# The last two down-projection tiles, the norm and the next mixer's first three tiles in halves of 128 tokens

## The chip, the cores and the metric

The kernel runs on one core of a Trainium2 chip. The metric is the time of one execution on the device in microseconds (us); several executions are timed and their median is compared.

## The reference, cut to what matters

A sequence of 256 tokens with 1024 channels goes through two stacks. The first (two blocks) is not touched. The second ("second layer" in the title) has four blocks, each a mixer and a feed-forward part, both followed by a residual and a layer norm:

```python
def swiglu(x, w_in, w_down):
    gate, up = jnp.split(x @ w_in, 2, axis=-1)
    return (jax.nn.silu(gate) * up) @ w_down

for i in range(4):                      # gated delta net, hgrn2, gla, gated delta net
    m = mixer_i(x)                      # begins with x @ w_in
    x = layer_norm(DN_ALPHA * x + m, mix_ln_g[i], mix_ln_b[i])
    x = layer_norm(DN_ALPHA * x + swiglu(x, ffn_w_in[i], ffn_w_down[i]), ffn_ln_g[i], ffn_ln_b[i])
return x
```

The hidden width is 2816, so the down projection contracts 22 blocks of 128 rows. The layer norm takes mean and variance over the 1024 channels of each token, so tokens are independent of each other in it. All is float32.

## The kernel before, in words

Activations are held transposed: channels on the 128 partitions, tokens along the free axis. `X` holds the residual stream as 8 channel tiles (`KC` = 8) of 256 tokens (`T`), `Xs` its split into a rounded part and a remainder in the reduced float32 type (float32r), 8 tiles each.

Every large projection is done by output tiles of 128 channels. `pe_block` (L595) makes one contraction block of one output tile with three matmuls: high weights by high activations (L597), high weights by low (L598), low weights by high (L599). Each matmul brings its own 128x128 weight load and streams 256 tokens. Weights arrive by DMA in `raw` (four slots, queue of SyncE), ScalarE rounds them to `w_hi` (L560, `split_hi`), VectorE subtracts to `w_lo` (L566, `split_lo`); both work some pieces ahead of TensorE.

`pe_ffn` (L690 on) does 44 up tiles and then the 8 down tiles; a down tile is 22 blocks in three pieces of 8, 8 and 6 (`PARTS`), so 66 matmuls. As each tile ends, VectorE adds the residual (`dve_residual`, L916), ScalarE squares it (L782), VectorE sums tiles and squares (L893, L897). After the last tile `pe_stats` multiplies these sums by a matrix of ones (L665, L666), then the last tile and its squares (L669, L671), in full float32. `pe_warm` issues five matmuls whose result nobody reads (L676), in the first three blocks only. Then `dve_ln` and `act_ln` (L843 to L881) form mean and reciprocal deviation and run a pipeline over the 8 channel tiles: centre (L849), scale (L853), gain and bias on ScalarE (L880 into `Xs`, L881 into `X`), remainder on VectorE (L870), which signals `h_ready` for one tile.

The next mixer begins with `pe_group`: its first three output tiles (`AHEAD` = 3) are advanced together, block k of all three as soon as `h_ready` has come for k, 72 matmuls in all. Its fourth tile follows when `lo_ready` says that its weights are split. After the last block ScalarE's queue stores the whole output with one DMA (L2940).

Three places join a feed-forward part to a mixer (blocks 0, 1 and 2); the fourth ends the program.

Of the kernel before, what the change touches and what calls it, by code (L numbers as in the profile page):

```python
# [147 lines left out]
def build(nc, a, out, stop=None):  # L148
    with ExitStack() as ctx:
# [19 lines left out]
        X = sb("X", [P, KC, 2 * T])  # L169
        M = sb("M", [P, KC, T])  # L170
        R = sb("R", [P, 8, 512])
        W = sb("W", [P, 8, 512])
        VC, NV = vector_columns()
        vec = sb("vec", [P, NV])
        ident, ones, halves, swap = (sb(n, [P, P]) for n in ("ident", "ones", "halves", "swap"))
        rope_cos, rope_sin = sb("rope_cos", [P, T]), sb("rope_sin", [P, T])
# [176 lines left out]
        for name, n, kind in plan:  # L353
# [4 lines left out]
            kinds += [kind] * n  # L358

        @block.sync  # L360
        def _(sp):
# [13 lines left out]
            for name, first, n, kind in [(name, *run, kind) for name, n, kind in plan for run in ORDER.get(name, ((0, n),))]:  # L375
# [156 lines left out]
        class Ahead:  # L532
# [21 lines left out]
        def split_hi(act, slot, fresh=False):  # L554
            if slot is None:
                return
            act.wait_ge(*loaded[slot].due("act", 16))
            if not fresh:
                act.wait_ge(*gemm_out.seen("act"))
            nc.scalar.activation(w_hi[:, slot], raw[:, slot], ACT.Identity).then_inc(*hi_ready.inc())  # L560

        def split_lo(dve, slot):
            if slot is None:
                return
            dve.wait_ge(*hi_ready.due("dve"))
            nc.vector.tensor_tensor(w_lo[:, slot], raw[:, slot], w_hi[:, slot], ALU.subtract).then_inc(*lo_ready.inc())  # L566

# [28 lines left out]
        def pe_block(to, w_slot, k, x_hi, x_lo, start, stop):  # L596
            nc.tensor.matmul(to, w_hi[:, w_slot, k, :], x_hi, start=start, stop=False)  # L597
            nc.tensor.matmul(to, w_hi[:, w_slot, k, :], x_lo, start=False, stop=False)  # L598
            return nc.tensor.matmul(to, w_lo[:, w_slot, k, :], x_hi, start=False, stop=stop)  # L599

# [15 lines left out]

        def pe_features(pe, tiles, n, ready=None):
# [8 lines left out]
            peel = SLOTS if ready or tiles == SLOTS else 0  # L626
            if ready:
                pe_group(pe, 0, n, ready)
            for u in range(AHEAD if ready else 0, peel):
# [60 lines left out]
        def pe_ffn(pe, n, stats, layer_norm=False, warm=5):  # L690
# [181 lines left out]
        def act_ln(act, which, i, split=True):  # L872
# [3 lines left out]
            for m in range(KC):  # L876
# [1085 lines left out]

        def pe_gdn(pe, i, ready):
            chunk = lambda t: slice(t * P, (t + 1) * P)
# [100 lines left out]

            pe_group(pe, 0, T, ready)
            for n in range(AHEAD, len(GDN_TILES)):
# [677 lines left out]

        def pe_hgrn(pe, ready):
            z = hgrn_
            pe_features(pe, 24, T, ready)
# [85 lines left out]

        def pe_gla(pe, ready):
            z = gla_
            pe_features(pe, 8, T, ready)
            for k in range(KC):
# [49 lines left out]
        @block.tensor  # L2888
        def _(pe):
            pe.wait_ge(*const_made.due("pe", 4))  # L2890
            pe_first(pe)
            if "ev_in" in names:
                pe_even(pe)
            if "up0" in names:
                pe_ffn0(pe)
            if "od_in" in names:
                pe_odd(pe)
            if "up1" in names:
                pe_ffn(pe, T, 0)
            for i, mixer in second:  # L2900
                if f"{mixer}_in" in names:
                    {"hgrn": pe_hgrn, "gla": pe_gla}.get(mixer, lambda e, r: pe_gdn(e, i // 3, r))(pe, pe_h(pe))
                if f"up_2_{i}" in names:
                    pe_ffn(pe, T, T, layer_norm=True, warm=5 if i < 3 else 0)

        @block.scalar
        def _(act):
# [21 lines left out]
            for i, mixer in second:  # L2929
# [4 lines left out]
                if f"up_2_{i}" in names:  # L2934
                    act_ffn(act, None, T)
                    act_squares(act, T, 3)
                    act_ln(act, "ffn", i, i < 3)
            if stop is None:
                act.wait_ge(*affine.sent())
                act.dma_start(out, Xl).then_inc(*stored.inc(16))  # L2940
                act.wait_ge(*stored.sent())

        @block.vector
        def _(dve):
# [29 lines left out]
            for i, mixer in second:  # L2974
# [123 lines left out]
```

## Time and profile before

| what | value |
|---|---|
| median of 3 runs | 2551.23 us (2549.55 to 2552.09) |
| profiled execution: first to last instruction (span) | 2545.7 us |
| median less that span | 5.5 us |
| TensorE matmuls busy | 2464.1 us, 97% |
| TensorE weight loads busy | 2261.9 us, 89% |
| VectorE, ScalarE busy | 1769.0 us, 1179.2 us |
| mean granted clock of TensorE | 0.988 |

The profiled execution has no time of its own beside its span; the 5.5 us are what the runs hold around the first and last instruction. PE is TensorE's matmuls, PEld its weight loads. A matmul in float32 appears as two records, each with a weight load of its own; one in float32r appears as one. Durations of matmuls overlap, so the pace of a stream is read from the distance between starts. The granted clock is 1.0 at 2.4 GHz and 0.5 at 1.2 GHz.

### The profile page before, as it was taken

Reading aid. Unit: us, or ns where it says so; the run is one execution under the profiler, and the core shown is the slowest. Engines: PE = TensorE matmul, PEld = TensorE weight load, DVE = VectorE, ACT = ScalarE, POOL = GpSimd, SP = SyncE. Lnnn points to the kernel's source line nnn. Section 1 sums busy time; section 2 is a strip of 40 time slices with the busy share of each in tenths; the row PEclk is TensorE's granted clock in tenths of the full one; section 3 lists DMA queues with packets and bytes.
Section 4 is the critical chain, followed back from the end, with each engine's and each line's share of the span. In section 5 each row is a group of like instructions: output and inputs, shape, how many; then the busy total and the mean of one; then the engine's idle time right before and its main releaser. Section 6 shows DMA issues by size and latency. Waiting matters only on the chain.

```text
span 2545.7 us, 46612 instructions
## 1 busy us (share of the span) xinstructions
PE 2464.1 (97%) x17610; PEld 2261.9 (89%) x17610; DVE 1769.0 (69%) x2863; ACT 1179.2 (46%) x1816; POOL 105.9 (4%) x161
## 2 busy tenths in 40 slices
PE   8999999999999999989999999999989999989998
PEld 6866777778798999988999998999989999988997
DVE  5878699988747866675665767666457657766665
ACT  4554421223545444455544544544545446455443
POOL 2221000000000000003000000000000000000000
PEclk9999999999999999999999999999999999999999
DMA  7323255554424554321555431555415554222553
GB/s 296 141 104 137 100 182 186 183 182 154 167 92 148 191 181 162 112 84 67 173 182 189 159 108 67 181 181 183 157 51 177 186 179 152 100 75 75 198 178 121
DMA packets 119641, 378.13 MB, mean 149 GB/s; under 512 B 11592, under 2 KB 29000, under 8 KB 119121
## 3 DMA queue, kind: packets, MB, share of 16 engines
q1 hardware_dynamic: 105936, 327.58, 38.1%
q0 software_dynamic: 12528, 47.62, 5.4%
q8 instruction: 94, 1.54, 0.2%
q10 hardware_dynamic: 1040, 1.05, 0.1%
q14 instruction: 43, 0.34, 0.0%
HBM read 375.15 MB, written 1.05 MB: 148 GB/s over the span
## 4 chain that ended last, share of the span: by engine, by line
PE 85%; DVE 9%; ACT 4%; issue 2%; DMA 0%; DVEq 0%; ACTq 0%; SPq 0%
PE gb L597 22%; PE gb L598 21%; PE gb L599 21%; DVE w_lo L566 3%; PE mb L676 2%; PE mb L2636 2%; PE gb L1162 1%; ACT w_hi L560 1%; PE gb L2617 1%; PE gb L2132 1%; PE mb L2150 1%; PE mb L599 1%; PE mb L598 1%; PE mb L597 1%; DVE W L2372 1%
## 5 line engine op out<-in xcount | busy, mean ns | idle before, releaser
L597 PE MATMUL gb<-Xs,w_hi 128*128 128x256 f32 (+1 forms) x3584 | 1098.3, 306 | 18.1 <-DVE w_lo L566 5.2
L599 PE MATMUL gb<-Xs,w_lo 128*128 128x256 f32 (+1 forms) x3584 | 1083.3, 302 | 0.0
L598 PE MATMUL gb<-Xs,w_hi 128*128 128x256 f32 (+1 forms) x3504 | 1053.4, 301 | 0.0
L560 ACT ACTIVATE w_hi<-raw 128x1024 fp32r<-128x1024 f32 x616 | 646.6, 1057 | 775.8 <-PE gb L599 730.6
L566 DVE TENSOR_TENSOR w_lo<-raw,w_hi 128x1024 fp32r<-128x1024 f32 x616 | 747.7, 1225 | 222.6 <-ACT w_hi L560 215.6
L597 PEld LDWEIGHTS gb<-Xs,w_hi 128*128 128x128 f32 x3584 | 679.0, 189 | 73.6 <-issue 29.9
L599 PEld LDWEIGHTS gb<-Xs,w_lo 128*128 128x128 f32 x3584 | 678.5, 189 | 31.2
L598 PEld LDWEIGHTS gb<-Xs,w_hi 128*128 128x128 f32 x3504 | 664.3, 190 | 26.4 <-issue 1.2
L598 PE MATMUL gb<-Fs,w_hi 128*128 128x256 f32 (+1 forms) x1016 | 294.4, 290 | 0.0
L597 PE MATMUL gb<-Fs,w_hi 128*128 128x256 f32 (+1 forms) x936 | 263.2, 281 | 0.0
L599 PE MATMUL gb<-Fs,w_lo 128*128 128x256 f32 (+1 forms) x936 | 261.9, 280 | 0.0
L598 PEld LDWEIGHTS gb<-Fs,w_hi 128*128 128x128 f32 x1016 | 190.9, 188 | 4.3 <-issue 0.2
L597 PEld LDWEIGHTS gb<-Fs,w_hi 128*128 128x128 f32 x936 | 175.8, 188 | 0.6 <-issue 0.2
L599 PEld LDWEIGHTS gb<-Fs,w_lo 128*128 128x128 f32 x936 | 175.9, 188 | 0.4
L994 ACT ACTIVATE W<-W 128x512 f32<-128x512 f32 (+1 forms) x44 | 23.1, 526 | 224.4 <-DVE W L953 224.4
L1269 DVE CUSTOM_DVE_ANT_0 R<-R,M 128x1024 f32<-128x1024 f32 x74 | 92.7, 1253 | 2.6
L1269 DVE CUSTOM_DVE_ANT_0 W<-R,M 128x1024 f32<-128x1024 f32 x74 | 92.3, 1248 | 0.1
L916 DVE SCALAR_TENSOR_TENSOR X<-X,gb 128x256 f32<-128x256 f32 x64 | 26.7, 417 | 92.0 <-PE gb L599 91.8
L2372 DVE SCALAR_TENSOR_TENSOR W<-gb,vec,W 128x255 f32<-128x255 f32 x96 | 46.1, 480 | 38.6 <-ACT W L2295 36.9
L964 DVE TENSOR_TENSOR W<-W,gb 128x256 f32<-128x256 f32 x110 | 46.1, 419 | 37.4 <-PE gb L599 37.2
L782 ACT ACTIVATE W<-X 128x256 f32<-128x256 f32 (+1 forms) x88 | 39.5, 448 | 63.5 <-DVE X L916 41.7
L474 POOL DMA_DIRECT2D R<-in_mod_later x80 | 42.6, 534 | 463.5 <-DVE modv L1273 395.0
(402 smaller groups left out, 2889.9 us busy)
## 6 DMA issues: line engine op xcount, KB each, us to landing
raw<-in_up SPq DMA_DIRECT2D x264, 512.0 KB, 3.8
raw<-in_down SPq DMA_DIRECT2D x96, 512.0 KB, 3.6
R<-in_mod_later POOLq DMA_DIRECT2D x80, 512.0 KB, 3.9
raw<-in_gdn_in SPq DMA_DIRECT2D x64, 512.0 KB, 3.6
raw<-in_down SPq DMA_DIRECT2D x48, 384.0 KB, 3.9
raw<-in_hgrn_in SPq DMA_DIRECT2D x32, 512.0 KB, 3.9
raw<-in_ev_in SPq DMA_DIRECT2D x24, 512.0 KB, 5.3
raw<-in_gla_in SPq DMA_DIRECT2D x24, 512.0 KB, 4.1
```

The source lines that it names most:

```text
L474: pool.dma_start(mod_ring[u], (a["mod_later"][t] if isinstance(t, int) else a["mod_later"][bass.ds(t, 1)].rearrange("a p n -> p (a n)"))). ...
L560: nc.scalar.activation(w_hi[:, slot], raw[:, slot], ACT.Identity).then_inc(*hi_ready.inc())
L566: nc.vector.tensor_tensor(w_lo[:, slot], raw[:, slot], w_hi[:, slot], ALU.subtract).then_inc(*lo_ready.inc())
L597: nc.tensor.matmul(to, w_hi[:, w_slot, k, :], x_hi, start=start, stop=False)
L598: nc.tensor.matmul(to, w_hi[:, w_slot, k, :], x_lo, start=False, stop=False)
L599: return nc.tensor.matmul(to, w_lo[:, w_slot, k, :], x_hi, start=False, stop=stop)
L676: nc.tensor.matmul(mb[:, 0, :], ones[:, :], vec[:, 0:512], start=True, stop=True)
L782: nc.scalar.activation(squares_at(m, n) if m else sq_sum(n), X[:, m, 0:n], ACT.Square, scale=1 / 32).then_inc(*sq_ready.inc())
L964: link(dve, nc.vector.tensor_tensor(g, g, bb, ALU.mult))
L1269: last = nc.vector.tensor_tensor_reduce(mod_ring[u] if s else product, mod_ring[u], c_rows[:, s, :], 1.0, 0.0, ALU.mult, ALU.add, sums[:, ...
L2372: link(dve, nc.vector.scalar_tensor_tensor(out=t[:, 3 - k:T], in0=a[:, 0:T - 3 + k], scalar=tap[k], in1=t[:, 3 - k:T], op0=ALU.mult, op1=A ...
L2636: last = nc.tensor.matmul(bank[:, b * 64:(b + 1) * 64], keys[:, b, :], queries[:, b * 64:(b + 1) * 64], start=True, stop=True)
```

## The change

In each feed-forward part of the second stack, down tiles 0 to 5 stay as they are. Tiles 6 and 7 (`HALVED`) are made for tokens 0 to 127 first (66 matmuls of 128 tokens each), then for tokens 128 to 255 (again 66 each). The split weights of both tiles must therefore be kept until the second pass: five of their six pieces (`ASIDE`) go to unused memory instead of the four slots. The statistics, the norm and the residual are done by halves (`stats`, `dve_ln_half`, `act_ln_half`), the first half's after four blocks of tile 6's second half. The norm walks over channels in chunks of 2, 2 and 4 tiles. The next mixer's first three tiles are done as 72 matmuls for the first half and 72 for the second (`pe_group_halves`), with the second half's statistics after the first two blocks. The five unread matmuls are gone from these places. The output is stored in four DMAs from SyncE's queue, two for each half. The first layer's parts and the norms after the mixers are not touched.

The diff, cut to its core (one level of indentation removed):

```diff
+HALVED = (KC - 2, KC - 1)
+ASIDE = (18, 21, 20, 22, 23)
+first_of = {name: sum(p[1] for p in plan[:j]) for j, (name, _, _) in enumerate(plan)}
+aside_of = {first_of[f"down_2_{i}"] + t: SLOTS + e for i in range(4) if f"down_2_{i}" in first_of for e, t in enumerate(ASIDE)}
+pairs = lambda z: z.rearrange("p (r b) n -> p r b n", b=2)
+def weights_at(w, part):
+    if w < SLOTS:
+        return (w_hi, w_lo)[part][:, w]
+    if w < SLOTS + 2:
+        return Rr[:, 2 * (w - SLOTS) + part]
+    if w == SLOTS + 2:
+        return spent[:, :, :] if part else Fs[:, FC:FC + 2, :].rearrange("p r (b n) -> p (r b) n", n=P)[:, 0:FC - WIDE]
+    r = 8 * (w - SLOTS - 3) + 4 * part
+    return Xs[:, r:r + 4, T:2 * T].rearrange("p r (b n) -> p r b n", b=2)
...
+    if stop is None:
+        for h in range(2):
+            for j in range(2):
+                cols, rows = slice(h * P, (h + 1) * P), slice(4 * j, 4 * j + 4)
+                sp.wait_ge(*final_made.due("sp", 1 if j else 2))
+                sp.dma_start(out[:, rows, cols], X[:, rows, cols]).then_inc(*stored.inc(16))
+        sp.wait_ge(*stored.sent())
...
+def pe_group_halves(pe, stats):
+    for u in range(AHEAD):
+        pe.wait_ge(*lo_ready.due("pe"))
+        pe.wait_ge(*gemm_taken.free("pe"))
+    for h, cols in enumerate(SIDES):
+        for k in range(KC):
+            pe.wait_ge(*h_ready.due("pe"))
+            for u in range(AHEAD):
+                last = pe_block(gb[:, u, cols], u, k, Xs[:, k, cols], Xs[:, KC + k, cols], k == 0, k == KC - 1)
+                if h and k == KC - 1:
+                    last.then_inc(*gemm_out.inc())
+            if h == 0 and k == 1:
+                stats(1)
...
+def pe_stats_half(pe):
+    def stats(h):
+        cols = SIDES[h]
+        pe.wait_ge(*sums_kept.due("pe"))
+        nc.tensor.matmul(mb[:, 2, cols], ones[:, :], x_sum[:, cols], start=True, stop=False)
+        nc.tensor.matmul(sbank[:, cols], ones[:, :], sq_sum(T)[:, cols], start=True, stop=False)
+        pe.wait_ge(*(gemm_taken.seen("pe", pe_next["tiles"]) if h else half_taken.due("pe")))
+        nc.tensor.matmul(mb[:, 2, cols], ones[:, :], X[:, KC - 1, cols], start=False, stop=True).then_inc(*mean_done.inc())
+        pe.wait_ge(*sq_ready.due("pe", 2 if h else KC))
+        nc.tensor.matmul(sbank[:, cols], ones[:, :], squares_at(KC - 1, T)[:, cols], start=False, stop=True).then_inc(*sum_done.inc())
+    return stats
+pe_next = {"tiles": 0}
+def pe_ffn_halves(pe, last_stage):
+    stats = pe_stats_half(pe)
+    pe_features(pe, 2 * FC, T, pe_h(pe))
+    def part_of(m, part, cols, first, end):
+        t = 3 * m + part
+        w = SLOTS + ASIDE.index(t) if t in ASIDE else t % SLOTS
+        for b in range(first, end):
+            k = KC * part + b
+            if m == 0:
+                pe.wait_ge(*gemm_taken.seen("pe", 2 * FC + 1 - 2 * (k + 1)))
+            last = pe_block(gb[:, m % BANKS, cols], w, b, hid[:, 0, k, cols], hid[:, 1, k, cols], k == 0, k == FC - 1)
+        return last
+    for m in range(KC):
+        pe.wait_ge(*gemm_taken.free("pe"))
+        for part, blocks in enumerate(PARTS):
+            pe.wait_ge(*lo_ready.due("pe"))
+            last = part_of(m, part, SIDES[0] if m in HALVED else slice(0, T), 0, blocks)
+            if m not in HALVED:
+                last.then_inc(*gemm_out.inc())
+        if m in HALVED:
+            last.then_inc(*half_out.inc())
+    for m in HALVED:
+        if m == HALVED[0]:
+            pe.wait_ge(*half_taken.due("pe"))
+        for part, blocks in enumerate(PARTS):
+            if m == HALVED[0] and part == 0:
+                part_of(m, part, SIDES[1], 0, 4)
+                stats(0)
+                last = part_of(m, part, SIDES[1], 4, blocks)
+            else:
+                last = part_of(m, part, SIDES[1], 0, blocks)
+            last.then_inc(*gemm_out.inc())
+    if last_stage:
+        pe_next["tiles"] = 0
+        stats(1)
+    pe_next["tiles"] = AHEAD
+    return stats
...
+CHUNKS = (slice(0, 2), slice(2, 4), slice(4, KC))
+def dve_ln_half(dve, h, split, beside=None):
+    cols, kept_cols = SIDES[h], slice(T + SIDES[h].start, T + SIDES[h].stop)
+    dve.wait_ge(*mean_done.due("dve"))
+    link(dve, nc.vector.tensor_scalar(W[:, 2, kept_cols], mb[:, 2, cols], 1.0 / D, None, ALU.mult))
+    nc.vector.tensor_tensor(W[:, 2, cols], W[:, 2, kept_cols], W[:, 2, kept_cols], ALU.mult).then_inc(*dve_step.inc())
+    dve.wait_ge(*sum_done.due("dve_sum"))
+    dve.wait_ge(*dve_step.sent())
+    nc.vector.tensor_tensor(W[:, 3, cols], sbank[:, cols], W[:, 2, cols], ALU.subtract).then_inc(*moments.inc())
+    spread = lambda z, ms: z.unsqueeze(1).broadcast_to([P, ms.stop - ms.start, P])
+    for ms in CHUNKS:
+        nc.vector.tensor_tensor(work[:, ms, cols], X[:, ms, cols], spread(W[:, 2, kept_cols], ms), ALU.subtract).then_inc(*centred.inc())
+    dve.wait_ge(*rstd_ready.due("dve"))
+    for ms in CHUNKS:
+        dve.wait_ge(*centred.due("dve"))
+        nc.vector.tensor_tensor(work[:, ms, cols], work[:, ms, cols], spread(W[:, 3, kept_cols], ms), ALU.mult).then_inc(*normed.inc())
+    for j, ms in enumerate(CHUNKS):
+        if beside and j == len(CHUNKS) - 1:
+            beside()
+        if split:
+            dve.wait_ge(*affine.due("dve"))
+            lo = slice(KC + ms.start, KC + ms.stop)
+            nc.vector.tensor_tensor(Xs[:, lo, cols], X[:, ms, cols], Xs[:, ms, cols], ALU.subtract).then_inc(*h_ready.inc(ms.stop - ms.start))
+def act_ln_half(act, i, h, split, beside=None):
+    cols, kept_cols = SIDES[h], slice(T + SIDES[h].start, T + SIDES[h].stop)
+    act.wait_ge(*moments.due("act"))
+    alink(act, nc.scalar.activation(W[:, 3, cols], W[:, 3, cols], ACT.Ln, bias=eps[:, 1:2]))
+    nc.scalar.activation(W[:, 3, kept_cols], W[:, 3, cols], ACT.Exp, scale=-0.5).then_inc(*rstd_ready.inc())
+    for j, ms in enumerate(CHUNKS):
+        if beside and j == len(CHUNKS) - 1:
+            beside()
+        act.wait_ge(*normed.due("act"))
+        for m in range(ms.start, ms.stop):
+            last = nc.scalar.activation(X[:, m, cols], work[:, m, cols], ACT.Identity, bias=vcol("ffn_b", KC * i + m),
+                                        scale=vcol("ffn_g", KC * i + m))
+        if split:
+            alink(act, last)
+            last = nc.scalar.activation(Xs[:, ms, cols], X[:, ms, cols], ACT.Identity)
+        last.then_inc(*(affine if split else final_made).inc())
+def act_down_halves(act, i, split):
...
+    def square(m, h):
+        cols = SIDES[h]
+        if h == 0:
+            act.wait_ge(*half_taken.due("act"))
+            act.wait_ge(*sq_added.due("act"))
+        else:
+            act.wait_ge(*gemm_taken.due("act"))
+        nc.scalar.activation(squares_at(m, T)[:, cols], X[:, m, cols], ACT.Square, scale=1 / 32).then_inc(*sq_ready.inc())
+    def split_next(n):
+        for _ in range(n):
+            split_hi(act, ahead["act"].next())
+    split_next(2)
+    square(HALVED[0], 0)
+    split_next(2)
+    square(HALVED[1], 0)
+    split_next(1)
+    act_ln_half(act, i, 0, split, beside=lambda: square(HALVED[0], 1))
+    square(HALVED[1], 1)
+    gemm_out.due("act", 2)
+    split_next(1)
+    gemm_out.due("act", 4)
+    act_ln_half(act, i, 1, split)
+    sq_added.due("act", 2)
+def dve_down_halves(dve, split):
...
+    def residual(m, h):
+        cols = SIDES[h]
+        if h:
+            dve.wait_ge(*gemm_out.due("dve", 3))
+            gemm_taken.due("dve")
+        else:
+            dve.wait_ge(*half_out.due("dve"))
+        nc.vector.scalar_tensor_tensor(out=X[:, m, cols], in0=X[:, m, cols], scalar=DN_ALPHA, in1=gb[:, m % BANKS, cols],
+                                       op0=ALU.mult, op1=ALU.add).then_inc(*(gemm_taken if h else half_taken).inc())
+    def sums(h):
+        cols = SIDES[h]
+        dve.wait_ge(*(gemm_taken.seen("dve") if h else half_taken.sent()))
+        dve.wait_ge(*x_added.sent())
+        nc.vector.tensor_tensor(x_sum[:, cols], x_sum[:, cols], X[:, HALVED[0], cols], ALU.add).then_inc(*x_added.inc())
+        dve.wait_ge(*sq_added.sent())
+        dve.wait_ge(*sq_ready.due("dve"))
+        nc.vector.tensor_tensor(sq_sum(T)[:, cols], sq_sum(T)[:, cols], squares_at(HALVED[0], T)[:, cols], ALU.add).then_inc(*sq_added.inc())
+        dve.wait_ge(*sq_added.sent())
+        dve.wait_ge(*x_added.sent())
+        nc.vector.memset(small[:, 156:157], 0.0).then_inc(*sums_kept.inc())
+        sq_ready.due("dve")
+    dve_tile(dve, 2)
+    residual(HALVED[0], 0)
+    sums(0)
+    dve_tile(dve, 2)
+    residual(HALVED[1], 0)
+    dve_tile(dve, 1)
+    def beside():
+        residual(HALVED[0], 1)
+        sums(1)
+    dve_ln_half(dve, 0, split, beside)
+    residual(HALVED[1], 1)
+    dve_ln_half(dve, 1, split)
...
-            {"hgrn": pe_hgrn, "gla": pe_gla}.get(mixer, lambda e, r: pe_gdn(e, i // 3, r))(pe, pe_h(pe))
+            if mixer == "hgrn":
+                pe_hgrn(pe, stats)
+            elif mixer == "gla":
+                pe_gla(pe, stats)
+            else:
+                pe_gdn(pe, i // 3, pe_h(pe), stats)
         if f"up_2_{i}" in names:
-            pe_ffn(pe, T, T, layer_norm=True, warm=5 if i < 3 else 0)
+            stats = pe_ffn_halves(pe, i == 3)
...
-            act_squares(act, T, 3)
-            act_ln(act, "ffn", i, i < 3)
-    if stop is None:
-        act.wait_ge(*affine.sent())
-        act.dma_start(out, Xl).then_inc(*stored.inc(16))
-        act.wait_ge(*stored.sent())
+            act_down_halves(act, i, i < 3)
...
-            dve_residual(dve, None, 0, T, 3, stats=T)
-            dve_ln(dve, split=i < 3)
+            dve_down_halves(dve, i < 3)
```

The lines left out hand a piece's destination through `split_hi`, `split_lo` and `pe_block` (`weights_at`), place the spare memory, and do tiles 0 to 5 as before.

## Rows read from the trace of the kernel before

**Rows 1.** The page: busy time (share of the span) of the engine, and the chain that ended last.
```profile
span 2545.7 us, 46612 instructions
PE 2464.1 (97%) x17610; PEld 2261.9 (89%) x17610; DVE 1769.0 (69%) x2863; ACT 1179.2 (46%) x1816; POOL 105.9 (4%) x161
PE 85%; DVE 9%; ACT 4%; issue 2%; DMA 0%; DVEq 0%; ACTq 0%; SPq 0%
```

**Rows 2.** Timeline of PE, block 0 to hgrn (start us, us, engine, line, what).
```profile
1395.97 0.59 PE L665 MATMUL mb<-W,ones 128*128 128x256 f32 x2
...
1397.70 4.46 PE L676 MATMUL mb<-vec,ones 128*128 128x512 f32 x10
1402.23 0.36 PE L597 MATMUL gb<-Xs,w_hi 128*128 128x256 f32 x1
1402.43 0.28 PE L598 MATMUL gb<-Xs,w_hi 128*128 128x256 f32 x1
...
1410.60 0.28 PE L599 MATMUL gb<-Xs,w_lo 128*128 128x256 f32 x1
1413.13 0.38 PE L597 MATMUL gb<-Xs,w_hi 128*128 128x256 f32 x1 [2.25 <-DVE w_lo L566]
```

**Rows 3.** Timeline of PE at the joint of block 2 and the last mixer.
```profile
2114.99 0.59 PE L665 MATMUL mb<-W,ones 128*128 128x256 f32 x2
...
2121.24 0.36 PE L597 MATMUL gb<-Xs,w_hi 128*128 128x256 f32 x1
```

**Rows 4.** Timeline of DVE, last two remainders of the same norm.
```profile
1407.59 0.42 DVE L870 TENSOR_TENSOR Xs<-X,Xs 128x256 fp32r<-128x256 f32 x1 [0.56 <-ACT X L881]
1408.57 0.43 DVE L870 TENSOR_TENSOR Xs<-X,Xs 128x256 fp32r<-128x256 f32 x1 [0.56 <-ACT X L881]
```

**Rows 5.** Weight loads by line: duration in ns min/median/max, first and last start.
```profile
L597 PEld LDWEIGHTS gb<-Xs,w_hi x3584: 186/188/333, 44.0 to 2468.6; 128*128 128x128 f32 x200
L2636 PEld LDWEIGHTS mb<-W x144: 187/192/193, 1515.9 to 1885.9; 128*128 128x128 f32 x144
L1162 PEld LDWEIGHTS gb<-Hn,silu_c x128: 81/85/129, 7.1 to 22.9; 128*2 128x2 f32 x128
L1170 PEld LDWEIGHTS mb<-ident,M x16: 133/136/138, 38.3 to 39.3; 2*128 2x128 f32 x16
```

**Rows 6.** Timelines of PEld and PE: streams of narrow matmuls, and two first float32r loads.
```profile
1884.32 1.95 PE L2636 MATMUL mb<-W 128*128 128x64 f32 x16
997.30 0.53 PEld L1980 LDWEIGHTS mb<-ones,W 128*128 128x128 f32 x4
38.33 1.15 PE L1170 MATMUL mb<-ident,M 2*128 2x2 f32 x16
1402.20 0.19 PEld L597 LDWEIGHTS gb<-Xs,w_hi 128*128 128x128 f32 x1 [0.88 <-issue]
1402.31 0.19 PEld L598 LDWEIGHTS gb<-Xs,w_hi 128*128 128x128 f32 x1
```

**Rows 7.** Windows of PE: start:end, length, PE busy (records), granted clock, DMA.
```profile
1414.20:1417.60 3.40, 3.40 (x19) 0.50 0.86 289
1880.80:1886.10 5.30, 5.30 (x50) 1.00 0.00 0
```

**Rows 8.** Timeline of PE: starts after 1414.2 us.
```profile
1414.56 0.42 PE L598 MATMUL gb<-Xs,w_hi 128*128 128x256 f32 x1
1414.77 0.42 PE L599 MATMUL gb<-Xs,w_lo 128*128 128x256 f32 x1
```

**Rows 9.** Timeline of the end, all engines, and two DMA issues (KB, us to landing).
```profile
2531.18 0.28 PE L599 MATMUL gb<-Fs,w_lo 128*128 128x256 f32 x1
2534.24 0.51 ACT L874 ACTIVATE W<-W,eps 128x256 f32<-128x256 f32 x1 [1.87 <-DVE W L857]
2535.69 4.78 ACT L881 ACTIVATE X<-W,vec 128x256 f32<-128x256 f32 x8 [0.49 <-DVE W L853]
...
out_x<-X ACTq DMA_DIRECT2D x1, 1024.0 KB, 4.8
vec<-in_vec SPq DMA_DIRECT2D x1, 370.5 KB, 3.2
```

More of the change, by code:

```diff
@@ L170, in build @@
         M = sb("M", [P, KC, T])
+        with nc.sbuf_tensor("Rr", [P, 4, KC, P], F32R) as Rr:
+            pass
         R = sb("R", [P, 8, 512])
@@ L174, in build @@
         vec = sb("vec", [P, NV])
-        ident, ones, halves, swap = (sb(n, [P, P]) for n in ("ident", "ones", "halves", "swap"))
+        ident, ones = (sb(n, [P, P]) for n in ("ident", "ones"))
+        with nc.sbuf_tensor("spent", [P, FC - WIDE, P], F32R) as spent:
+            pass
+        halves, swap = (sb(n, [P, P]) for n in ("halves", "swap"))
         rope_cos, rope_sin = sb("rope_cos", [P, T]), sb("rope_sin", [P, T])
@@ L263, in build @@
         silu_done = signal("silu_done")
+        half_out = signal("half_out")
+        half_taken = signal("half_taken")
+        final_made = signal("final_made")
         tap_done = signal("tap_done")
@@ L543, in next @@
                 slot = (self.at + self.n) % SLOTS if self.left > self.n else None
+                if slot is not None:
+                    slot = slot, aside_of.get(self.at + self.n, slot)
                 self.at += 1
@@ L556, in split_hi @@
                 return
+            slot, to = slot if isinstance(slot, tuple) else (slot, slot)
             act.wait_ge(*loaded[slot].due("act", 16))
-            if not fresh:
+            if not fresh and to < SLOTS:
                 act.wait_ge(*gemm_out.seen("act"))
-            nc.scalar.activation(w_hi[:, slot], raw[:, slot], ACT.Identity).then_inc(*hi_ready.inc())
+            hi = weights_at(to, 0)
+            nc.scalar.activation(hi, raw[:, slot, 0:hi.shape[1]] if len(hi.shape) == 3 else pairs(raw[:, slot]), ACT.Identity).then_inc(*hi_ready.inc())
         def split_lo(dve, slot):
@@ L596, in pe_block @@
         def pe_block(to, w_slot, k, x_hi, x_lo, start, stop):
-            nc.tensor.matmul(to, w_hi[:, w_slot, k, :], x_hi, start=start, stop=False)
-            nc.tensor.matmul(to, w_hi[:, w_slot, k, :], x_lo, start=False, stop=False)
-            return nc.tensor.matmul(to, w_lo[:, w_slot, k, :], x_hi, start=False, stop=stop)
+            nc.tensor.matmul(to, weight_block(w_slot, 0, k), x_hi, start=start, stop=False)
+            nc.tensor.matmul(to, weight_block(w_slot, 0, k), x_lo, start=False, stop=False)
+            return nc.tensor.matmul(to, weight_block(w_slot, 1, k), x_hi, start=False, stop=stop)
         def rows_of(k, n):
@@ L615, in pe_group, with pe_features @@
                         last.then_inc(*gemm_out.inc())
-        def pe_features(pe, tiles, n, ready=None):
+        SIDES = (slice(0, P), slice(P, T))
+        def pe_group_halves(pe, stats):
[11 more added lines that the diff above has]
+                        stats(1)
+        def pe_features(pe, tiles, n, ready=None, halves=None):
             def tile(u):
@@ L624, in tile @@
                 last.then_inc(*gemm_out.inc())
-            peel = SLOTS if ready or tiles == SLOTS else 0
+            peel = SLOTS if ready or halves or tiles == SLOTS else 0
             if ready:
                 pe_group(pe, 0, n, ready)
-            for u in range(AHEAD if ready else 0, peel):
+            if halves:
+                pe_group_halves(pe, halves)
+            for u in range(AHEAD if ready or halves else 0, peel):
                 tile(u)
@@ new lines, in dve_down_halves @@
+        def dve_down_halves(dve, split):
+            for m in range(HALVED[0]):
+                dve_tile(dve, 2)
+                dve.wait_ge(*gemm_out.due("dve", 3))
+                gemm_taken.due("dve")
+                nc.vector.scalar_tensor_tensor(out=X[:, m, 0:T], in0=X[:, m, 0:T], scalar=DN_ALPHA, in1=gb[:, m % BANKS, 0:T],
+                                               op0=ALU.mult, op1=ALU.add).then_inc(*gemm_taken.inc())
+                dve_sums(dve, m, T, True)
+                dve_tile(dve, 2 if m == HALVED[0] - 2 else 1)
+            def residual(m, h):
+                cols = SIDES[h]
+                if h:
+                    dve.wait_ge(*gemm_out.due("dve", 3))
+                    gemm_taken.due("dve")
+                else:
[17 more added lines that the diff above has]
+            sums(0)
+            dve_tile(dve, 2)
+            residual(HALVED[1], 0)
[6 more added lines that the diff above has]
+            dve_ln_half(dve, 1, split)
@@ L1961, in dve_picks, with pe_gdn @@
             nc.vector.reduce_sum(pick_sub[:, :], ident[:, :].rearrange("p (n b) -> p b n", b=NSUB), AX_X).then_inc(*picks_made.inc())
-        def pe_gdn(pe, i, ready):
+        def pe_gdn(pe, i, ready, halves=None):
             chunk = lambda t: slice(t * P, (t + 1) * P)
@@ L2064, in turn_values @@
                 last.then_inc(*v_turned.inc())
-            pe_group(pe, 0, T, ready)
+            if halves:
+                pe_group_halves(pe, halves)
+            else:
+                pe_group(pe, 0, T, ready)
             for n in range(AHEAD, len(GDN_TILES)):
@@ L2743, in dve_gla_core, with pe_hgrn @@
             gn_dve_out(dve, z.items, z.parts)
-        def pe_hgrn(pe, ready):
+        def pe_hgrn(pe, halves):
             z = hgrn_
-            pe_features(pe, 24, T, ready)
+            pe_features(pe, 24, T, halves=halves)
             pe_tokens(pe, 4, T)
@@ L2833, in build, with pe_gla @@
         gate_log32 = M[:, 0:4, :].rearrange("p a c -> p (a c)").rearrange("p (t n) -> p t n", t=TC)
-        def pe_gla(pe, ready):
+        def pe_gla(pe, halves):
             z = gla_
-            pe_features(pe, 8, T, ready)
+            pe_features(pe, 8, T, halves=halves)
             for k in range(KC):
```

16 lines of the change are left out of this document (15 added, 1 removed).

## The prediction

> **What bounds the kernel now.** I read the page first. TensorE's matmuls are busy 97% of the 2545.7 us span, its weight loads 89%, and 85% of the chain that ended last is TensorE [rows 1]. So there are two ways to gain: shorten the matmul streams, or close the holes between them. This change aims at holes, so the timeline around a joint comes next [rows 2]. At the end of block 0 the last down matmul hands over at 1395.97 (start of the statistics) and the next mixer's first matmul starts at 1402.23: 6.26 us, of which 1.73 are statistics (1395.97 to 1397.70) and the rest unread matmuls and waiting for the norm. The joint of block 2 shows 2121.24 - 2114.99 = 6.25 [rows 3], and I take block 1's as the same. After 72 group matmuls the mixer of block 0's joint stands again, 1410.60 to 1413.13, for `w_lo` [rows 2]. In the last block nothing follows: the last down matmul starts at 2531.18, the span ends at 2545.7 [rows 9]. That is all the change can win: three joints, one stall, one tail.
>
> **What the price hangs on.** The edit also turns 256-token matmuls into twice as many of 128 tokens. At a joint, two down tiles (132 matmuls) become 264, the group's 72 become 144; the last block has the 132 alone. In all 3 x 204 + 132 = 744 matmuls become 1488. From 1402.43 to 1410.60 the group's records 2 to 72 make 70 steps in 8.17 us: 117 ns each [rows 2]; so today's work is 744 x 0.117 = 87.0 us. If time followed tokens, halves would cost 58.5 ns and nothing would be added. But each half brings a whole 128x128 weight load, and the trace shows what a stream of narrow matmuls costs. At L2636, 64 tokens wide in float32, the 16 records take 1.95 us in a merged row, the last of them about 0.28 (the length of the matmul records in [rows 2]): (1.95 - 0.28) / 15 = 111 ns apart. At L1980, one column wide, four loads take 0.53, the last 0.19: 0.34 / 3 = 113 ns [rows 6]. A width of 64 or of 1 changes nothing, so the load sets that pace. Is a float32r load faster? Its record is 188 ns long against 192 in float32; a load of 2 columns takes 85 [rows 5], so the length does grow with the columns loaded, 103 ns for 126 of them, and both types are on that line. And where TensorE had been waiting, the first two float32r loads of a group start 1402.20 and 1402.31, 110 ns apart [rows 6], with no stream ahead of them to hold the second back. I therefore take 111 ns for each half matmul; bounds of this case 108 (just the load, read off the 103 ns for 126 columns and the starts) and 117 (as today's). The float32r matmul of 128 tokens itself is nowhere in the trace, so I keep 58.5 below and, above, 223 (two records of 112 ns for one matmul, as float32 has).
>
> **Sum of the streams.** 1488 x 0.111 = 165.2 us, less 87.0: +78.1 us. By parts: two down tiles 29.3 for 15.4, four times, +55.4; group 16.0 for 8.4, three times, +22.7. With 108 ns it is +73.7, with 117 +87.1. All of it is on TensorE, which is the path.
>
> The Trainium skill, page "TensorE: Matmul & The Clock Gate", section "Back-to-back issue gap", gives about 81 ns per matmul for a sustained stream of loads and matmuls of 128 columns. By it the halves would take 1488 x 0.081 = 120.5 us, +33.5 and not +78.1. It is not the row's number, and the narrow streams here stand at 111 and 113, so I do not take it.
>
> **Joints.** After the change the statistics are two sets of four float32 matmuls, eight records each, at 0.112: 0.9 us each, 1.8 a joint. The first set's norm runs beneath tile 6's and 7's second halves. From statistics to the first group matmul today's norm takes 1402.23 - 1397.70 = 4.5 us, and it then gives one 256-token tile each 0.98 us [rows 4]; a half I take at 4.5 for the first and 0.6 per tile after. Stat set 0 ends 2.2 us into 14.7 us of second halves, so 8 tiles are there by 2.2 + 4.5 + 4.8 = 11.5. Its last chunk stands behind residual and sums of tile 6 on VectorE and its square on ScalarE (`beside`), which come at 8.3; then four gains, one rounding and one remainder: about 3.5 us, ready at 12, still ahead. The second set is put after two blocks of the group's first half; it waits for tile 7's residual and square (0.3 + 0.4 + 0.4 us after the tile, from the lengths before) under 18 matmuls, 2.0 us. Its norm then has 54 matmuls of cover, 6.0 us, against 4.5, and the second half takes a block each 1.0 us against 0.6 made. No wait is left at these rates. So each joint saves 6.26 - 1.8 = 4.5 us: -13.4 us. Queued behind the waits are only the group's own matmuls on TensorE and the next split on VectorE.
>
> **The stall after hgrn's group.** `w_lo` for the fourth tile was late because VectorE finished the norm at 1409.0 and then had small work [rows 2, 4]. Now the norm is over some 5 us before the 16 us group ends, so the 2.53 - 0.12 = 2.4 us go. Behind that stall the granted clock is 0.50 for 3.4 us [rows 7], starts 0.21 us apart and not 0.117 [rows 8], which costs 16 x 0.095 = 1.5 us; I let it go too: -3.9 us (bounds 0 and -3.9).
>
> **The tail.** Today 2545.7 - 2531.30 = 14.4 us: 2.9 to ScalarE's first step at 2534.24, 1.45 to the first gain at 2535.69, 4.8 for eight gains, 5.2 for the store (4.8 to landing) [rows 9]. With half the width, an instruction lies between half and all of its length; taking 0.7 of it gives 2.1, 1.4 (the scaling now waits for three centre steps), and 3.3. Of four stores three go under the work; the last is 256 KB. The nearest row, 370.5 KB in 3.2 us [rows 9], gives 3.6 with its issue. Sum 10.4, saves 4.0, but set 0 of the statistics adds 0.9 to TensorE: -3.1 us (bounds -1 and -6).
>
> **Costed at nothing.** Weight loads from memory go by `lo_ready`, as before, and have the longer streams as cover. The splits are the same number; keeping five pieces aside only lets them come earlier. The four stores are issued by SyncE, whose loads have ended.
>
> **The sum.** +78.1 - 13.4 - 3.9 - 3.1 = +57.7 us on a span of 2545.7, the 5.5 us around it unchanged: 2551.2 + 57.7 = 2609 us, 2.3% slower. With 108 ns and all savings at their high bound 2601; with 117 and the low ones 2624.
>
> **Rivals.**
> *Load not the limit.* The array swaps float32r weights as fast as it streams them, and a half costs 58.5 to 61 ns. For it: L1170's loads, also 128 columns, are 136 long, not 188, and its stream runs at about (1.15 - 0.2) / 15 = 63 ns [rows 5, 6], so neither issue nor the load path forbids it. Against: float32r's 188 and the 110 ns between its first loads. Then the streams add 0 to 3.7 us, but the norm loses cover: the second half's first tile comes 4.5 us after its statistics, 54 matmuls give 3.2, and production at 0.6 falls behind 0.53 a block; I charge 2.5 us a joint, 7.5. 2551.2 + 2 - 20.4 + 7.5 = 2540. This is the one on the other side; it decides below (87.0 + 12.9) / 1488 = 67 ns.
> *Part of the load hidden.* Between 67 and 104 ns a half, the streams' surplus is 13 to 68 us. At 81 ns it gives 2551.2 + 33.5 - 20.4 + 2 = 2566. That is the case of the skill's section above; no row has such a spacing.
> *Halves in two records, or at the low clock.* If float32r of 128 tokens is made as float32 is, a half costs 223 ns: +331.8 - 87.0 - 20.4 = +224, 2776 us. If the clock fell to 0.50 through these streams, 213 ns: 2761. Against the clock: 48 records of 64 tokens ran at 1.00 [rows 7], whose array is as idle between loads as these halves'; but that is 5.3 us, and here it is 45 us on end. Single falls of 3.4 us cost 1.6 each; eight would be 13, which the upper end takes in. For two records nothing in the trace speaks, nor against.
>
> **Chances.** Forecast (104 to 118 ns) 0.75, its own range 2599 to 2625; partly hidden 0.05; load not the limit 0.09; two records or low clock 0.11. The range has to leave out no more than 2 in 10: 2556 to 2625 holds the forecast and the partly hidden load. A measurement of this kernel tells about 0.2% from no change, 5 us. Faster by more: 0.09; within: 0.01; slower: 0.90.
>
> **What would show it.** In the changed trace: the distance between starts of L598-like matmuls 128x128 in the halves (111 ns right, 58 wrong); about 29 us for the two tiles and 16 for the group; the joint without a hole beyond two statistics; no wait for `w_lo` after hgrn's group; one record per half matmul; granted clock 1.00 there; the last store landing some 10 us after the last down matmul. The prediction is wrong if the spacing is not the load's.

## The result and the profile after

The changed kernel takes 2606.31 us (median of 4, 2601.99 to 2614.87) against 2551.31 us. The ratio over all runs is 1.0229, 95% interval 1.0214 to 1.0243 (the two medians alone give 1.0216): 2.3% slower. Its profiled execution took 2602.65 us and has a span of 2600.9 us, 55.2 more than before [rows 1]. So a run holds only 1.8 us around its first and last instruction; in all later runs it is 1.6 to 1.8. Of the 5.5 us between median and span of before, the rest must be that the profiled execution was faster than the median one, as it is here (2606.31 - 2600.9 = 5.4).

The page: span, busy time and share of it by engine, chain.

```profile
span 2600.9 us, 48174 instructions
PE 2525.1 (97%) x18356; PEld 2332.1 (90%) x18356; DVE 1773.2 (68%) x2873; ACT 1186.2 (46%) x1858; POOL 106.2 (4%) x161
PE 84%; DVE 9%; ACT 3%; issue 2%; DMA 1%; SPq 0%; DVEq 0%; ACTq 0%
```

TensorE is the bound as before and 61 us busier; VectorE and ScalarE are 4 and 7 us busier. Now the timeline of PE around the first joint, to be laid beside [rows 2]: the last whole matmuls and the first halves of tile 6, the hand-over to the group, the second statistics, and the group's end.

```profile
1379.26 0.28 PE L641 MATMUL gb<-Fs,w_lo 128*128 128x256 f32 x1
1379.37 0.22 PE L639 MATMUL gb<-Fs,Rr 128*128 128x128 f32 x1
...
1409.47 0.27 PE L640 MATMUL gb<-Fs,Xs 128*128 128x128 f32 x1
1409.59 0.27 PE L641 MATMUL gb<-Fs,Xs 128*128 128x128 f32 x1
1409.70 0.27 PE L639 MATMUL gb<-Xs,w_hi 128*128 128x128 f32 x1
1409.81 0.28 PE L640 MATMUL gb<-Xs,w_hi 128*128 128x128 f32 x1
...
1411.71 0.43 PE L756 MATMUL mb<-W,ones 128*128 128x128 f32 x2
...
1412.57 0.30 PE L639 MATMUL gb<-Xs,w_hi 128*128 128x128 f32 x1
...
1426.56 0.27 PE L641 MATMUL gb<-Xs,w_lo 128*128 128x128 f32 x1
1426.67 0.33 PE L639 MATMUL gb<-Xs,w_hi 128*128 128x256 f32 x1
```

The hole of 6.26 us is gone: the group's first matmul follows the last down matmul by 0.11. So is the stall before the fourth tile (1426.56 to 1426.67). But the steps between half matmuls are 0.11 us, and whole matmuls ahead of them have 0.12: half the tokens, nearly the same time. One matmul in float32r is one record, also at 128 tokens.

Windows of PE over the two halved tiles and over the halved group of this joint (length, busy and records, granted clock, DMA):

```profile
1379.40:1409.60 30.20, 30.20 (x274) 1.00 0.41 134
1409.70:1426.60 16.90, 16.90 (x154) 1.00 0.04 8
```

The clock stayed at 1.00, against what [rows 7] show behind the old stall. The end, all engines, to be laid beside [rows 9]:

```profile
2591.14 0.28 PE L641 MATMUL gb<-Fs,Xs 128*128 128x128 f32 x1
2591.26 0.44 PE L756 MATMUL mb<-W,ones 128*128 128x128 f32 x2
...
2593.37 0.40 ACT L1031 ACTIVATE W<-W,eps 128x128 f32<-128x128 f32 x1 [1.28 <-DVE W L1011]
...
2594.97 3.19 ACT L1038 ACTIVATE X<-W,vec 128x128 f32<-128x128 f32 x8 [0.86 <-DVE W L1018]
2596.65 1.91 SPq L455 DMA_DIRECT2D out_x<-X  x2
```

The stores in the list of DMA issues (count, KB each, median us to landing):

```profile
out_x<-X SPq DMA_DIRECT2D x4, 256.0 KB, 2.3
```

From the start of the closing statistics (2591.26) to the end of the span it is 9.7 us, where it was 14.4.

### The profile page after: what moved, and what is told of

It is laid out like the page before. It is cut to its first block, busy times and chain, and to the rows that moved or that the text cites. A ratio compares the mean times of both kernels' runs of the same rounds, so it can differ in the third digit from the quotient of the medians.

```text
span 2600.9 us, 48174 instructions
## 1 busy us (share of the span) xinstructions
PE 2525.1 (97%) x18356; PEld 2332.1 (90%) x18356; DVE 1773.2 (68%) x2873; ACT 1186.2 (46%) x1858; POOL 106.2 (4%) x161
## 4 chain that ended last, share of the span: by engine, by line
PE 84%; DVE 9%; ACT 3%; issue 2%; DMA 1%; SPq 0%; DVEq 0%; ACTq 0%
PE gb L639 22%; PE gb L640 22%; PE gb L641 22%; DVE w_lo L608 2%; PE mb L2884 1%; PE mb L737 1%; ACT w_hi L600 1%; PE gb L2865 1%; PE gb L2380 1%; PE mb L2398 1%; PE mb L640 1%; PE mb L641 1%; PE mb L639 1%; DVE W L2620 1%; DMA Pj<-in_mod 1%
## 5 line engine op out<-in xcount | busy, mean ns | idle before, releaser
L639 PE MATMUL gb<-Xs,w_hi 128*128 128x256 f32 (+2 forms) x3656 | 1116.7, 305 | 15.7 <-DVE Xs L925 3.9
L641 PE MATMUL gb<-Xs,w_lo 128*128 128x256 f32 (+2 forms) x3656 | 1101.4, 301 | 0.0
L640 PE MATMUL gb<-Xs,w_hi 128*128 128x256 f32 (+2 forms) x3576 | 1071.2, 300 | 0.0
L600 ACT ACTIVATE w_hi<-raw 128x1024 fp32r<-128x1024 f32 x596 | 625.0, 1057 | 741.9 <-PE gb L641 696.7
L608 DVE TENSOR_TENSOR w_lo<-raw,w_hi 128x1024 fp32r<-128x1024 f32 x596 | 724.1, 1224 | 231.5 <-ACT w_hi L600 223.6
L639 PEld LDWEIGHTS gb<-Xs,w_hi 128*128 128x128 f32 x3656 | 692.6, 189 | 68.4 <-issue 26.9
L640 PEld LDWEIGHTS gb<-Xs,w_hi 128*128 128x128 f32 x3576 | 677.7, 190 | 26.1 <-issue 1.2
L640 PE MATMUL gb<-Fs,w_hi 128*128 128x256 f32 (+2 forms) x904 | 262.3, 290 | 0.0
L639 PE MATMUL gb<-Fs,w_hi 128*128 128x256 f32 (+2 forms) x824 | 231.5, 281 | 0.0
L641 PE MATMUL gb<-Fs,w_lo 128*128 128x256 f32 (+2 forms) x824 | 230.3, 280 | 0.0
L640 PEld LDWEIGHTS gb<-Fs,w_hi 128*128 128x128 f32 x904 | 170.1, 188 | 4.3 <-issue 0.2
L639 PEld LDWEIGHTS gb<-Fs,w_hi 128*128 128x128 f32 x824 | 155.1, 188 | 0.6 <-issue 0.2
L641 PEld LDWEIGHTS gb<-Fs,w_lo 128*128 128x128 f32 x824 | 155.1, 188 | 0.4
L1211 DVE TENSOR_TENSOR Fs<-W,Fs 128x256 f32 x110 | 46.8, 426 | 15.7
```

The lines of the kernel that those rows point to most:

```text
L600: nc.scalar.activation(hi, raw[:, slot, 0:hi.shape[1]] if len(hi.shape) == 3 else pairs(raw[:, slot]), ACT.Identity).then_inc(*hi_ready.inc())
L608: nc.vector.tensor_tensor(lo, raw[:, slot, 0:hi.shape[1]] if len(hi.shape) == 3 else pairs(raw[:, slot]), hi, ALU.subtract).then_inc(*lo_r ...
L639: nc.tensor.matmul(to, weight_block(w_slot, 0, k), x_hi, start=start, stop=False)
L640: nc.tensor.matmul(to, weight_block(w_slot, 0, k), x_lo, start=False, stop=False)
L641: return nc.tensor.matmul(to, weight_block(w_slot, 1, k), x_hi, start=False, stop=stop)
L1211: nc.vector.tensor_tensor(hid[:, 1, jj, :], g, hid[:, 0, jj, :], ALU.subtract).then_inc(*gemm_taken.inc(2))
```

## The experiments

Joint lengths below are from the start of the last down matmul to the start of the next mixer's fourth tile, read from the timelines: before 17.3, 14.9 and 14.9 us; changed kernel 17.1 at each. They hold the group but not the two halved down tiles. Each ratio is against runs of the kernel before made beside the experiment; their medians were 2548.68 us for e1 to e4, 2548.79 for e5 to e8, and 2547.01 for e9 and e10. The edits are shown shortened.

**Half of each weight load taken away (e1_load64).**

```diff
+hi, lo = weight_block(w_slot, 0, k)[:, 0:64], weight_block(w_slot, 1, k)[:, 0:64]
-pe_block(gb[:, u, cols], ...)            # halves only; the same in the down tiles
+pe_block_narrow(gb[0:64, u, cols], ...)
```

> The changed kernel, but in every half matmul (128 tokens) only 64 of the 128 weight columns are loaded and used; the other 64 output channels of these tiles are left out. If the weight load sets the pace of the halves (theory), the load falls from about 107 to 54 ns, the 128-token stream needs 53, and starts come 58 to 64 ns apart in place of 111: 1488 x 0.05 = 74 to 79 us less streaming, some 7 us of it lost to waits for the norm whose cover is gone: 2530 to 2540 us, below the kernel before. If a narrow float32r matmul has a price of its own that the load doesn't make (rival: slow streaming below 256 tokens, or issue), the spacing stays at 111 ns and the time at 2606 us.

Measured: 2546.87 us, ratio to before 0.9996 (0.9984 to 1.0009). Weight loads of one line (ns min/median/max):

```profile
L646 PEld LDWEIGHTS gb<-Xs,w_hi x144: 133/135/139, 1399.6 to 2131.8; 128*64 128x64 f32 x144
```

Timeline of PE in the halves and at the first joint:

```profile
1385.14 0.22 PE L646 MATMUL gb<-Fs 128*64 128x128 f32 x1
1385.20 0.22 PE L647 MATMUL gb<-Fs,spent 128*64 128x128 f32 x1
...
1398.83 0.22 PE L647 MATMUL gb<-Fs,Xs 128*64 128x128 f32 x1
1399.59 0.24 PE L645 MATMUL gb<-Xs,w_hi 128*64 128x128 f32 x1 [0.54 <-DVE X L1105]
```

The waits of PE from tile 6's first half to the fourth tile (us, times, longest):

```profile
PE gb L645 <- DVE Xs L1031: 2.2, 2, 1.2
PE gb L639 <- DVE w_lo L608: 1.7, 1, 1.7
PE mb L765 <- DVE X L1105: 1.6, 1, 1.6
PE gb L645 <- DVE X L1105: 0.5, 1, 0.5
```

The load went from 188 to 192 ns down to 135 and the spacing of the same 128-token matmuls from 112 to 60 (medians of all 1488). The number of instructions and the tokens streamed stayed; with the load only the output channels were halved, and the next run shows that a smaller output alone does not shorten the step. So the load sets the pace. The waits add up: 6.0, 4.5 and 5.1 us came back at the three joints (1.7 of the first for the weights of the fourth tile, the rest for residual and norm), 15.6 in all where I had allowed 7.5. That is 8 us more, and the time is 7 us above the expected stretch.

**Half of each stream taken away (e2_tokens64).**

```diff
+some = slice(cols.start, cols.start + 64)
-pe_block(gb[:, u, cols], u, k, Xs[:, k, cols], Xs[:, KC + k, cols], ...)
+pe_block(gb[:, u, some], u, k, Xs[:, k, some], Xs[:, KC + k, some], ...)
```

> The changed kernel, but every half matmul streams only the first 64 of its 128 tokens; the products of the other 64 tokens of each half are left out. If the load sets the pace, the spacing stays at 111 ns and the time at 2606 us (2600 to 2612). If the stream sets it, at half speed below 256 tokens (rival), the spacing falls to about 56 to 60 ns and the time to about 2535 us.

Measured: 2749.92 us, ratio 1.0789 (1.0767 to 1.0810); neither expectation of the time came true. Timeline of PE early in the first halved tile and 16 us on:

```profile
1384.20 0.28 PE L640 MATMUL gb<-Fs,Rr 128*128 128x64 f32 x1
1384.31 0.28 PE L641 MATMUL gb<-Fs,Rr 128*128 128x64 f32 x1
...
1400.18 0.40 PE L640 MATMUL gb<-Fs,Xs 128*128 128x64 f32 x1
1400.40 0.40 PE L641 MATMUL gb<-Fs,Xs 128*128 128x64 f32 x1
```

Windows of PE over the same stretch:

```profile
1382.90:1387.50 4.60, 4.60 (x44) 1.00 0.67 222
1387.70:1468.00 80.30, 80.30 (x379) 0.50 0.13 43
```

While the clock was at 1.00 the 64-token matmuls stood 0.11 us apart, as the 128-token ones do: the stream's length does not matter, as expected. But then the granted clock fell to 0.50 and stayed there to the end of the halves, with steps of 0.21; this in all four places, and it accounts for the 144 us. The prediction's rival of the low clock is thus a real mechanism, at half the width that the change uses.

**High weights loaded once for two products (e3_paired).**

```diff
+both = gb[:, bank, :].rearrange("p (a t) -> p a t", a=2)[:, :, cols]
+nc.tensor.matmul(both, hi, x, ...)                     # x = [high | low], 2 x 128 tokens
+nc.tensor.matmul(gb[:, bank, cols], lo, x[:, 0, :], ...)
```

> The changed kernel, but in the halved down tiles the high weights are loaded once for high and low activations together (one matmul of 2 x 128 tokens into both halves of the bank, the low product added by VectorE with the residual). Output complete. Two loads for each half block in place of three: (117 + 111) against 333 ns, 352 half blocks, so 37 us less if loads are what is paid: about 2569 us, still slower than before. If the number of tokens streamed were what is paid, nothing would change: 2606 us.

Measured: 2569.58 us, ratio 1.0081 (1.0061 to 1.0101). The timeline of PE in a halved down tile:

```profile
1389.68 0.33 PE L649 MATMUL gb<-Fs,Xs 128*128 128x256 f32 x1
1389.85 0.22 PE L650 MATMUL gb<-Fs,Xs 128*128 128x128 f32 x1
1389.91 0.34 PE L649 MATMUL gb<-Fs,Xs 128*128 128x256 f32 x1
```

A half block has a period of 0.23 us in place of 0.33, with the same products. By the timelines the two halved down tiles take 21.3 us at each of the four places where the changed kernel has 30.3: 36 us fewer, and 37 were expected. The times agree: 0.0229 - 0.0081 = 0.0148, or 38 us. The number of loads is what is paid.

**The group left whole (e4_group_whole), and the unread matmuls put back (e9_group_whole_warm).**

```diff
+stats(1)
+pe_warm(pe, 5)                                         # in e9 only
-for h, cols in enumerate(SIDES): for k in range(KC): ...
+for k in range(KC):
+    pe.wait_ge(*h_ready.due("pe", 1 if k else KC + 1))
+    ... pe_block(gb[:, u, 0:T], ...)
```

> The changed kernel, but the next mixer's first three tiles are made in whole matmuls of 256 tokens, after the second half's statistics and norm. The theory: the group falls from 16.0 to 8.4 us and 5.0 us of waiting for the norm come back, so each of three joints gains 2.5 to 3 us: 2598 us. The rival, that halving the group pays by itself because it covers the norm's 4.5 us: slower than 2606 us.

> The kernel of the whole group (down tiles in halves, group whole), with the five unread 512-wide matmuls of before put back behind the second half's statistics. If that kernel missed its 2598 us because the granted clock fell to 0.50 for 6.8 us in the hole at each of three joints, the clock now stays at 1.00 there and about 2 to 3 us a joint come back: 2594 to 2598 us, and no low clock behind the three joints in the profile. If it is the wait for the norm that is longer than taken, nothing changes: 2603 us.

Measured: e4 2603.00 us, ratio 1.0210 (1.0193 to 1.0227); e9 2600.44 us, ratio 1.0214 (1.0197 to 1.0231). Both are above what was expected (2598, and 2594 to 2598), and by the times neither can be told from the changed kernel nor from the other. The profiles can tell, for the joints alone. Windows of PE after the three joints in e4:

```profile
1414.00:1420.80 6.80, 4.38 (x20) 0.51 0.00 0
1806.50:1813.30 6.80, 4.41 (x20) 0.51 0.01 2
2161.50:2168.30 6.80, 4.62 (x21) 0.51 0.00 0
```

And in e9:

```profile
1412.00:1418.00 6.00, 6.00 (x23) 1.00 0.00 0
1805.00:1811.00 6.00, 6.00 (x43) 1.00 0.01 3
2160.00:2166.00 6.00, 6.00 (x47) 1.00 0.01 3
```

The joint is 16.3 us in e4 and 14.3 in e9, where the changed kernel has 17.1 and before 14.9 (without its stall). So halving the group costs 2.8 us a joint more than it hides, provided that something holds the clock in the hole. The whole execution does not show these 8 us: the spans of the changed kernel and of e9 differ by 3.3, and the mean granted clock is 0.989 in the one and 0.986 in the other, so e9 lost more to falls of the clock elsewhere.

**The unread matmuls alone (e10_no_unread).**

```diff
-pe_ffn(pe, T, T, layer_norm=True, warm=5 if i < 3 else 0)
+pe_ffn(pe, T, T, layer_norm=True, warm=0)
```

> The kernel before without the five unread matmuls at the three joints and nothing else. The change removed them too, and its TensorE had work there. If they hold the clock in the 4.5 us hole of before, the clock falls to 0.50 for some 6.8 us at each joint and 2 to 3.4 us a joint are lost: 2555 to 2559 us. If they hold nothing: 2549 us, the same.

Measured: 2553.76 us, ratio 1.0027 (1.0012 to 1.0043). Timeline of PE at the first joint:

```profile
1400.93 0.59 PE L671 MATMUL mb<-W,ones 128*128 128x256 f32 x2
1405.90 0.44 PE L597 MATMUL gb<-Xs,w_hi 128*128 128x256 f32 x1 [4.37 <-DVE Xs L870]
1406.14 0.42 PE L598 MATMUL gb<-Xs,w_hi 128*128 128x256 f32 x1
```

Windows of PE behind all three joints:

```profile
1405.00:1409.00 4.00, 3.10 (x15) 0.63 0.00 0
1781.00:1785.00 4.00, 3.90 (x20) 0.57 0.00 0
2122.00:2126.00 4.00, 3.46 (x17) 0.60 0.01 2
```

The clock falls for one stretch of 3.4 us a joint, not 6.8; the second and third joint are 16.4 us long, not 14.9. The first is unchanged at 17.3: it has its fall earlier, and its stall is then 1.0 us long, not 2.5, with no fall behind it. The unread matmuls hold the clock; the changed kernel could do without them only because its halves keep TensorE at work.

**The change in the last block alone (e5_last_only).**

```diff
-stats = pe_ffn_halves(pe, i == 3)
+stats = pe_ffn_halves(pe, True) if i == 3 else pe_ffn(pe, T, T, layer_norm=True)
```

> The kernel before with the change in the last block alone (two down tiles in halves, norm by halves, four stores); the three joints are as before. The theory: 13.9 us more streaming, 3 to 5 us less tail: 9 to 11 us slower than before, 2561 us. The rival, that the last block's part pays because norm and store of the first half go under TensorE's work: not slower than 2551 us.

Measured: 2558.16 us, ratio 1.0044 (1.0029 to 1.0058): 9 us slower by the medians, 11 by the ratio. The steps in its halves are 112 ns, its tail 9.7 us from the start of the last down matmul against 14.5. Even where no group follows and three of the four stores are issued before the last gain is done, the halves cost more than they give.

This profile has one thing more to show. Its first joint is that of the kernel before, stall included, but the granted clock stays at 1.00 behind it. Timeline and window of PE:

```profile
1414.97 0.28 PE L641 MATMUL gb<-Xs,w_lo 128*128 128x256 f32 x1
1417.51 0.38 PE L639 MATMUL gb<-Xs,w_hi 128*128 128x256 f32 x1 [2.27 <-DVE w_lo L608]
1417.60:1421.00 3.40, 3.40 (x29) 1.00 0.67 202
```

So the fall that [rows 7] show behind the same stall comes in some executions and not in others.

**Two gains without halves (e6_stores, e7_hgrn_early_split, e8_both).**

```diff
-act.dma_start(out, Xl)                                           # e6, e8
+for j in range(4):                                               # SyncE's queue
+    sp.wait_ge(*final_made.due("sp", 2))
+    sp.dma_start(out[:, 2*j:2*j+2, :], X[:, 2*j:2*j+2, 0:T])
 last.then_inc(*dve_a.inc())                                      # dve_hgrn: e7, e8
+dve_tile(dve)
 dve.wait_ge(*act_a.due("dve"))
```

> The kernel before with one part of the change's idea and none of its price: the output goes in four stores from SyncE's queue, each of two channel tiles of all 256 tokens, as the last norm finishes them; no halves. The last store moves 256 KB, which took 2.3 us to land in the changed kernel against 4.8 us for 1024 KB: 2.5 us faster, 2549 us. The rival, that a store's time lies in its fixed part and the queue's issue: no difference.

> The kernel before, but in the second mixer VectorE splits the fourth tile's weights ahead of most of its small work on the forget-gate bounds. If the 2.5 us stall behind the group is VectorE's order alone, 2 us of it go, and with it the fall of the clock to 0.50 behind it (1.5 us, perhaps a second one later, 1.6): 3.5 to 5 us faster, 2546 to 2548 us. If the clock falls there anyway: 2549 us. If TensorE then waits for ScalarE instead: no difference.

> The kernel before with the four stores by channel tiles and the earlier split in the second mixer together, no halves. If both gains are on the path and independent, they add: 6 to 7.5 us faster, about 2544 us, faster than both kernels. If not: no better than the better of the two alone.

Measured: e6 2547.32 us, ratio 0.9996 (0.9984 to 1.0008); e7 2543.93 us, 0.9987 (0.9975 to 0.9998); e8 2541.27 us, 0.9980 (0.9969 to 0.9991). Timeline of ScalarE and SyncE at e6's end:

```profile
2539.10 4.78 ACT L887 ACTIVATE X<-W,vec 128x256 f32<-128x256 f32 x8 [0.49 <-DVE W L859]
2540.22 4.06 SPq L425 DMA_DIRECT2D out_x<-X  x4
```

Timeline of PE at the second mixer's fourth tile in e7:

```profile
1413.17 0.27 PE L599 MATMUL gb<-Xs,w_lo 128*128 128x256 f32 x1
1413.68 0.39 PE L597 MATMUL gb<-Xs,w_hi 128*128 128x256 f32 x1 [0.24 <-DVE w_lo L566]
```

In e6 the gains end at 2543.88 and the span at 2546.7: 2.8 us, where [rows 9] have 5.2. That gain of 2.4 us is in the profile, but below what the times can tell. In e7 the stall is 0.51 us and not 2.53, and the joint is 15.2 us, not 17.3; 3.5 to 5 us were expected, the ratio gives 3 (1 to 6). Together they make the kernel 0.2% faster than before, 5 us by the ratio (2 to 8) and 7.5 by the medians. That the two add up (6 to 7.5 us) is therefore neither shown nor excluded. e8 has the lowest time of all kernels here, but its interval overlaps that of e7.

## Why the prediction was right

**Price of a half matmul.** Taken 111 ns, from float32 streams of other widths and the length of loads. Measured over the first joint: 1426.67 - 1379.37 = 47.30 us, less two sets of statistics of 1412.57 - 1411.71 = 0.86, over 408 matmuls: 112 ns. That it is the load is shown by e1 (half the load, 60 ns), e2 (half the stream, still 0.11 us while the clock was up) and e3 (a third of the down tiles' loads gone, and nearly a third of their time). The rival of a partly hidden load, 67 to 104 ns, is excluded by the 112. With the last block's 29.4 us the halves take 3 x 45.6 + 29.4 = 166.2 us, against 165.2 forecast and 87.0 before: +79.2 for +78.1.

**Joints.** 6.26 - 1.72 = 4.5 us saved at each, 13.6 in all for the 13.4 forecast. TensorE waited for nothing at the three joints.

**Stall and clock.** The stall's 2.4 us went. From that joint to the next block's down tiles, two falls of the clock are missing and the stretch is 3.2 us shorter: 300.2 us (1413.13 to 1713.34) became 297.0 (1426.67 to 1723.72). I had counted 1.5 for one fall and put it down to the change. That part isn't shown. The code of this stretch is the same in both kernels, and e5 and e10, whose first joint is not halved, take 296.5 us for it; e5 has the stall and no fall, and the second fall, some 90 us on, is there in e3 and e7 and missing in e5, e6 and e10. Such falls come and go with the execution.

**Tail.** 14.4 became 9.7; less the extra statistics 3.8 us saved, forecast 3.1. Its parts are 2.1, 1.6 and 3.2 us to the last gain, forecast 2.1, 1.4 and 3.3, and 2.7 from there to the end (2598.16 to 2600.9), forecast 3.6: the nearest row for the store landed in 3.2, these four in 2.3.

**Sum.** +79.2 - 13.6 - 2.4 - 3.2 - 3.8 = +56.2, and 1.2 us less before the first joint, makes +55.0; the spans differ by 55.2. Forecast +57.7. The agreement to 0.2 us is partly luck: two later stretches are 0.6 and 1.0 us longer, the six whole down tiles of two blocks 0.4 us shorter each, and the -3.2 cannot be put down to the change. Without it the change costs some 58 us.

**Where the text was off.** The first rival, a load that does not limit, was priced at 2540 us. e1 is nearly that case (60 ns), and it took 2547: I charged 2.5 us a joint for the lost cover, and 4.5 to 6 came back. The price from which the change pays is therefore lower than the 67 ns given. At 60 ns it only comes out even, because the norm then takes longer than the shortened work covers. That rival rested on L1170's loads, 128 columns and steps of 63 ns; they have 2 rows of weights where the halves have 128, and no run shows why their steps are shorter.

The low-clock rival was right as a mechanism and wrong for 128 tokens: the granted clock is 1.00 through the halves at all four places. What I held against it was weak, though. The 5.3 us of narrow float32 records at 1.00 say little, for e2's streams too ran 4 to 6 us at 1.00 before their clock fell. Here the right outcome was in part luck. That streams of 128 tokens kept the clock and streams of 64 lost it is shown; nothing between them was run. The spread of the changed kernel's executions goes with their mean granted clock (0.989 at 2602 us, 0.985 at 2615), as single falls would have it; only one of them has a trace.

## What to carry to other kernels

Before splitting a matmul along its tokens, read the spacing of the narrowest stream in the trace: if it does not shrink with width, every split buys a second weight load at full price, here 112 ns for each, and 4.5 us of waiting saved at a joint cost almost 22 us of added loads. Put the hidden latency beside the count of added loads first; a small reordering on the engine that was late (one split ahead of small work) took some 3 us off this kernel, where the whole rebuild added 55. And when a hole is left, keep something in it that holds TensorE's clock.

## What the runs showed of the hardware

A stream of 64-token float32r matmuls, busy without a gap by the profile, kept a granted clock of 1.00 for 4.6 us, then lost it and ran at 0.50 for 80 us on end (e2); one of 128 tokens with the same loads kept 1.00 for 47 us. TensorE's busy share was 100% in both. A load of 64 weight columns in float32r is 135 ns long and lets matmuls start every 60 ns (e1), one of 128 columns 188 to 192 and 112. In e3 a matmul streams 2 x 128 tokens from two places of memory into two places of a bank. The next one starts 0.17 us after it and the one behind that 0.06 later: the pair's sum is 0.23, about what two loads of 0.11 would give.
